# The first stage of a two-layer hybrid decoder step in two channel halves, with one group of modulation products moved in front of the first projection

## Chip, cores and metric

The kernel runs on one core of a Trainium2 chip, as a single launch. The metric is the device time of that launch in microseconds (us). Engines are named as the profile names them: PE is the tensor engine (PEld its weight loads), DVE the vector engine, ACT the scalar engine, POOL the GpSimd engine, SP the sync engine, which issues most DMAs. "ACTq" and "SPq" are the queues in which ACT and SP issue DMAs.

## The reference

Two layers run one after the other over a prompt of 512 positions and 8 single decode steps, 520 columns in all, with 1024 channels. What matters here is the beginning of a layer:

```python
mod = silu(c) @ ada_w + ada_b                 # c: 9 conditioning rows (8 samples, 1 prompt)
shift, scale, gate = split(mod, 3)
h = rms_norm(x, norm_g) * (1.0 + scale) + shift
proj = h @ w_in                               # 30 tiles of 128 columns for four mixers, then gate tiles
```

Then four mixers (RWKV-7, retention, RG-LRU, gated DeltaNet) work on slices of proj, each result is gated and lifted back to 1024 channels, the four are merged, multiplied by w_out and added to x. A last rms_norm ends the second layer. All states are written out as well. Everything is fp32, and the large products are made from two parts (a rounded part, hi, and the rest, lo): hi*hi + lo*hi + hi*lo.

## The kernel before

**Layout.** Channels lie on the 128 partitions: xT, h_hi and h_lo are [128, 8, 520], one block of 128 channels for each of the 8 middle indices. h_hi is laid over xT and h_lo over hT (`sb_parts`), so h_hi may only be written when xT is no longer needed, and xT has to be stored (scr_x) for the residual at the layer's end.

**The start (lines 346 to 470).** SP issues, in this order: the conditioning rows, the first constants, parameters, x (2 MB in four DMAs), the first two thirds of layer 0's ada_w (8 MB in eight DMAs of 1 MB, two for each of four groups b = 0..3 of 512 columns), the first three tiles of w_in into the ring (`first_load`), the store of xT in two halves, the remaining constants and the tree masks. Groups 0 and 1 are the shift of channel blocks 0 to 3 and 4 to 7, groups 2 and 3 their scale. PE transposes x into xT, sums the squares of the 8 blocks with a matrix of ones (line 458, [128,128] weights, all 128 output rows alike), and makes the four groups of modulation products (`ada_products`, line 311: 32 instructions for a group, on four column groups of 32 columns). ACT copies each group's rows out of PSUM (line 390) and PE turns them into columns (`mod_columns`, line 318). ACT also makes rs = exp(-0.5 ln(mean square + eps)) (lines 385, 387), and then the hi parts of the first two tiles of w_in (`first_split`, line 299), whose second waits for the second tile's load. When all four groups are there, DVE makes modT (line 418) and G = (1 + scale) * norm_g (line 420).

**Layer loop.** DVE makes hT = xT * G * rs for the 8 decode columns (lines 1965 to 1970) and block by block for the prompt (lines 1968, 1977), ACT adds the shift and rounds to h_hi (lines 1608, 1609), and DVE makes h_lo (lines 1974, 1980). In front of that ACT waits until the stores of xT have landed. PE makes tiles 0 and 1 of proj together, block by block: `product` splits a tile into 12 parts, 0 to 7 the blocks with the hi weights against h_hi and h_lo (line 881), 8 to 11 the lo weights (line 889), two blocks each:

```python
for p in range(KT):
    proj(0, [p])
    proj(1, [p])
for idx in range(2):
    proj(idx, range(KT, PARTS))
```

From tile 2 on PE takes a tile at a time. A weight tile is loaded by SP into one of three ring slots once the tile that had the slot is done, ACT makes its hi part (line 1540) right after it has evacuated the tile two places before (`evac`, line 1555), and POOL its lo part in two halves (line 717). All order is written out by hand: each engine's program is a fixed list, and waits are on step counters (`Track`). SP goes through the tiles in order, and `before` puts other transfers in front of given loads; in front of proj 3's load stand the wait for the last modulation step, four DMAs of a decode state and two copies of conv states (lines 526, 615, 616). After its eight h_hi steps ACT issues nine small DMAs (lines 1612 to 1620: state rows, two LoRA weights, gate weights, two small vectors), then evacuates tile 0. Both layers do this.

**Activation tables.** Where ACT needs a function that the table set loaded at that point lacks, a table load stands before the instruction. Ln and Exp follow each other in rs (lines 385 and 387 at the start, 1934 and 1936 at the join of the layers, 1926 and 1929 at the very end), in `norm` (lines 1591, 1593, three times a layer) and at lines 1657 and 1659, and each of the two has a table load of its own.

Of the kernel before, what the change touches and what calls it, by code (L numbers as in the profile page):

```python
# [4 lines left out]
D_MODEL, SEQ, DEPTH, NB = 1024, 512, 2, 8  # L5
HEADS, HD = 4, 64
# [71 lines left out]
def build_program(nc, a, o, order):  # L78
# [8 lines left out]
    with ctx:  # L87
# [52 lines left out]
        rows0 = [RC[:, b, 0:256] for b in range(4)]  # L140
        sq0 = [mg5[:, 2], mg5[:, 3], mg5[:, 4], tg[:, 1], ws[:, 14], ws[:, 15], ws[:, 16], ws[:, 17]]
# [77 lines left out]
        class Layer:  # L219

            def __init__(self, n):
                names = ("states_in", "small_weights_in", "outputs_written", "shift_rows_written", "decode_states_written", "scratch_written",
                         "decode_vectors_in", "decode_states_in", "decode_rows_in", "x_saved")
                (self.st, self.w2, self.out, self.crow, self.so, self.scr, self.vec, self.ss, self.oread, self.xout) = (sem(f"{name}{n}") for name in names)
# [120 lines left out]

        block = ctx.enter_context(nc.Block())
        @block.sync
        def _(sp):
# [9 lines left out]
            for e in range(8):  # L358
                sp.dma_start(pairs[e], a["ada_w"][0, 512 * (e % 2):512 * (e % 2) + 512, 512 * (e // 2):512 * (e // 2) + 512]  # L359
                             .rearrange("(k p) c -> p k c", p=P)).then_inc(s_ada0[e], 16)  # L360
# [15 lines left out]
        def _(act):  # L376
            A = nc.scalar.activation
            act.wait_ge(s_c, 48)
            A(mg5[0:9, 0:2, 0:512], RC[0:9, 2:4, 0:512], ACT.Tanh, scale=0.5).then_inc(*act0.step("tanh_c"))
            for d in range(KT):  # L380
                act.wait_ge(*dve0.at("x", d))
                A(sq0[d], xT[:, d, :], ACT.Square).then_inc(*act0.step("sq"))
            act.wait_ge(s_const, 32)
            act.wait_ge(*pe0.at("ss"))
            A(rs.rearrange("p (h c) -> p h c", h=2), psB[:, 2:4, 0:HALF], ACT.Ln, bias=cc("eps"), scale=1.0 / D_MODEL).then_inc(*act0.step("ln"))
# [9 lines left out]
        def _(dve):  # L395
# [17 lines left out]
            for d in range(KT):  # L413
                dve.wait_ge(*pe0.at("x", d))
                nc.vector.tensor_copy(xT[:, d, 0:SEQ], psA[:, d % 4, :]).then_inc(*dve0.step("x"))
# [2277 lines left out]
```

## Time and profile before

| | us |
|---|---|
| runs (3), median | 1380.09 |
| lowest, highest | 1377.6, 1385.19 |
| the profiled execution | 1379.26 |
| its span in the profile | 1377.4 |
| PE busy in the span | 1323.3 |
| DVE, ACT, POOL busy | 623.8, 450.6, 373.7 |

The profiled execution is one more run of the same program. Its own time is 1.9 us more than the span from its first to its last recorded instruction. In the timeline, each row is: start in us from the span's start, duration, engine, source line, operation, output<-input by the program's names, shapes, and the number of instructions merged in the row; in brackets how long the engine was idle before it and what released it. Durations of merged rows run from the first start to the last end. PE's rows overlap, since matmuls are pipelined.

### The profile page before, as it was taken

How to read it: one execution, taken by the hardware profiler on the slowest of the kernel's cores; microseconds unless marked ns; L12 is line 12 of the kernel's file. 1: busy time of each engine (PE TensorE's matmuls, PEld its weight loads, DVE VectorE, ACT ScalarE, POOL GpSimd, SP SyncE). 2: the span in 40 equal slices, each digit the busy share in tenths (PEclk: the TensorE clock that was granted, in tenths of full speed). 3: DMA queues.
4: the chain of work that ended last, by engine and by line, in shares of the span. 5: the costliest groups of instructions: out<-in, count | busy, mean ns of one | idle time of the engine just before them, and what ended most of it. 6: DMA issues, size and time to landing. Idle time of an engine off the chain costs nothing.

```text
span 1377.4 us, 39970 instructions
## 1 busy us (share of the span) xinstructions
PE 1323.3 (96%) x18146; PEld 1195.7 (87%) x18146; DVE 623.8 (45%) x1158; ACT 450.6 (33%) x742; POOL 373.7 (27%) x286
## 2 busy tenths in 40 slices
PE   6699999999999999999979999999999999999996
PEld 4699999899899999887779999999988999988795
DVE  2648514318234326656242972242543242565643
ACT  3333522234322235231143252222542223533123
POOL 0244421123222232120333442222331222322121
PEclk9899999999999999999989999999999999999998
DMA  8733231125431272578843323212273224545932
GB/s 318 237 93 89 77 95 49 44 70 123 120 85 49 64 135 82 155 194 266 284 148 91 92 78 86 59 47 64 76 165 85 64 57 90 127 132 135 291 113 93
DMA packets 275933, 162.60 MB, mean 118 GB/s; under 512 B 86102, under 2 KB 244922, under 8 KB 275252
## 3 DMA queue, kind: packets, MB, share of 16 engines
q1 hardware_dynamic: 273556, 158.01, 41.5%
q8 instruction: 143, 2.34, 0.7%
q10 hardware_dynamic: 2208, 2.03, 0.5%
q14 instruction: 26, 0.21, 0.1%
HBM read 135.25 MB, written 24.89 MB: 116 GB/s over the span
## 4 chain that ended last, share of the span: by engine, by line
PE 87%; ACT 3%; SPq 3%; DVE 3%; DMA 3%; issue 1%; ACTq 1%; DVEq 0%
PE psA L881 38%; PE psA L889 19%; PE psA L931 7%; PE psB L807 2%; PE psB L823 2%; PE psB L827 1%; DMA ring<-in_ada_w 1%; SPq L359 1%; PE psB L1006 1%; PE psB L311 1%; PE psB L1016 1%; SPq L293 1%; DMA upw<-in_w_up 1%; PE psB L791 1%; PE psB L1244 1%
## 5 line engine op out<-in xcount | busy, mean ns | idle before, releaser
L717 POOL TENSOR_TENSOR w_lo<-ring,w_hi 128x512 fp32r<-128x512 f32 x248 | 329.9, 1351 | 832.6 <-ACT w_hi L1540 790.2
L881 PE MATMUL psA<-h_hi,w_hi 128*128 128x260 f32 x1984 | 427.1, 297 | 17.7 <-DVE h_lo L1974 16.5
L881 PE MATMUL psA<-h_lo,w_hi 128*128 128x260 f32 x1984 | 402.5, 285 | 0.0
L881 PEld LDWEIGHTS psA<-h_hi,w_hi 128*128 128x128 f32 x1984 | 307.8, 190 | 37.4 <-issue 26.8
L881 PEld LDWEIGHTS psA<-h_lo,w_hi 128*128 128x128 f32 x1984 | 309.0, 190 | 0.2
L889 PE MATMUL psA<-h_hi,w_lo 128*128 128x260 f32 x1984 | 273.3, 286 | 0.0
L889 PEld LDWEIGHTS psA<-h_hi,w_lo 128*128 128x128 f32 x1984 | 248.9, 187 | 6.8 <-issue 3.0
L1540 ACT CAST w_hi<-ring 128x1024 fp32r<-128x1024 f32 x120 | 123.8, 1032 | 9.7 <-DMA ring<-in_w_in 9.6
L832 ACT COPY ws<-psB 128x128 f32<-128x128 f32 x80 | 21.5, 269 | 186.8 <-PE psB L807 159.9
L1570 ACT ACTIVATE tg<-psA 128x520 f32<-128x520 f32 x48 | 28.9, 603 | 124.8 <-PE psA L889 124.6
L840 DVE COPY_PREDICATED tg<-tmask,psB 128x128 f32<-128x128 uint8 x40 | 14.3, 356 | 101.2 <-PE psB L827 57.6
L840 DVE COPY_PREDICATED ws<-tmask,psB 128x128 f32<-128x128 uint8 x40 | 14.3, 357 | 79.0 <-PE psB L827 42.4
L717 POOL TENSOR_TENSOR rb_lo<-RB,w_hi 128x512 fp32r<-128x512 f32 x16 | 21.7, 1375 | 101.4 <-ACT w_hi L1540 101.4
L717 POOL TENSOR_TENSOR rb_lo<-RB,ra_lo 128x512 fp32r<-128x512 f32 x16 | 21.0, 1338 | 47.8 <-ACT ra_lo L1540 47.8
L931 PE MATMUL psA<-RB,upw 128*128 128x260 f32 x128 | 31.9, 393 | 1.2 <-DMA upw<-in_w_up 1.0
L1555 ACT COPY RA<-psA 128x520 f32<-128x520 f32 x18 | 10.7, 594 | 66.3 <-PE psA L889 66.3
L2229 DVE SCALAR_TENSOR_TENSOR ws<-RD,parT,ws 128x511 f32<-128x511 f32 (+2 forms) x36 | 30.9, 923 | 0.7 <-ACT ws L1744 0.6
L931 PEld LDWEIGHTS psA<-RB,upw 128*128 128x128 f32 x128 | 23.1, 190 | 9.3 <-issue 6.0
L931 PE MATMUL psA<-RA,upw 128*128 128x260 f32 x128 | 30.7, 385 | 0.0
L931 PE MATMUL psA<-RD,upw 128*128 128x260 f32 x128 | 29.9, 384 | 0.8 <-DVE RA L2030 0.8
L931 PE MATMUL psA<-RC,upw 128*128 128x260 f32 x128 | 30.0, 387 | 0.0
L889 PE MATMUL psA<-merged_hi,rb_lo 128*128 128x260 f32 x224 | 29.1, 282 | 0.0
(495 smaller groups left out, 1981.8 us busy)
## 6 DMA issues: line engine op xcount, KB each, us to landing
ring<-in_w_in SPq DMA_DIRECT2D x122, 512.0 KB, 4.2
ring<-in_ada_w SPq DMA_DIRECT2D x32, 512.0 KB, 5.6
scr_tanh<-tg SPq DMA_DIRECT2D x48, 260.0 KB, 4.6
upw<-in_w_up SPq DMA_DIRECT2D x64, 128.0 KB, 3.6
RB<-in_w_out SPq DMA_DIRECT2D x16, 512.0 KB, 3.9
RA<-scr_tanh SPq DMA_DIRECT2D x30, 260.0 KB, 4.0
ws<-scr_tanh SPq DMA_DIRECT2D x24, 260.0 KB, 4.3
xT<-scr_x SPq DMA_DIRECT2D x8, 520.0 KB, 5.1
```

The costliest lines, as they stand in the source:

```text
L293: sp.dma_start(RS[s], a["w_in"][layer, :, col:col + P].rearrange("(k p) c -> p k c", p=P)).then_inc(arrived, 16)
L717: nc.gpsimd.tensor_tensor(tile_part(RL[s][:, k], (kind, n)), tile_part(RS[s][:, k], (kind, n)), tile_part(HS[L.hslot[q]][:, k], (kind, n)) ...
L807: last = nc.tensor.matmul(meet(z0[pr, cols], lv, 0), At[pr, q, cols], meet(T4[pr, q, cols], lv, 0), start=True, stop=True)
L823: nc.tensor.matmul(meet(z0[pr, cols], lv, 0), V4[pr, q, cols], meet(Y4[pr, q, cols], lv, 0), start=True, stop=True)
L832: nc.scalar.copy(meet(q64(Y), lv, 0), meet(q64(psB[:, 2, 0:256]), lv, 0)).then_inc(*ta.step("y"))
L840: nc.vector.copy_predicated(meet(q64(T), lv, 0), bc(meet(tmask[:, lv, :], lv, 0), 1, 4), meet(q64(psB[:, 2, 0:256]), lv, 0))
L881: nc.tensor.matmul(out(h), HS[L.hslot[q]][:, p, 0:m], cols(part(p), h), start=(p == 0 and part is hi), stop=False)
L889: last = nc.tensor.matmul(out(h), RL[s][:, k, 0:m], cols(hi(k), h), start=False, stop=(k == KT - 1))
L931: last = nc.tensor.matmul(out(hf), upw[:, idx % UP_RING, i, :], outs[MERGE[idx][0]][:, i, hf * HALF:(hf + 1) * HALF], start=(i == 0), stop ...
L1540: nc.scalar.copy(tile_part(HS[L.hslot[q]], SPLIT[q]), tile_part(RS[s], SPLIT[q])).then_inc(*aw.step("hi"))
L1570: A(half(th_tile(idx)), psA[:, b:b + 2, 0:HALF], ACT.Tanh, scale=0.5).then_inc(*am.step("th"))
L2229: last = STT(out[:, t, sh:SEQ], raw[:, t, 0:SEQ - sh], par(wname, tap * n + t), out[:, t, sh:SEQ], mult, add)
```

## The change

- The start works in two halves of four channel blocks. x goes to two other places (`x0`: RC and mg5) instead of xT, so h_hi no longer lies over it, and each half is stored from there with a semaphore of its own. ACT's wait for the stores is gone from layer 0's start; SP and ACT wait for them where RC and mg5 are used again.
- Order of ada_w groups: 0, 2, 1, 3 on SP and on PE. SP's first three ring loads stand between them.
- The sum of squares: ones with 32 columns, block d on column group d % 4, then a DVE copy of the four partial sums and one more product with ones over it (the scale gets a factor 1/32).
- PE: group 0, the last product for the sums, group 2, columns of both, group 1; then, inside layer 0's loop over blocks in front of block 4, group 3, the columns of groups 1 and 3, and parts 8 and 9 of tiles 0 and 1.
- DVE makes modT, G, the decode columns and hT for each half by itself.
- POOL waits in layer 0 for h_lo of block 3 before its first lo part.
- The nine small DMAs are issued by SP in both layers, at the head of the layer's list; in layer 0 behind the wait for the last modulation step.
- ACT loads a table set (`natural_log_exp_and_others`) by hand: after the first tanh, after the squares in `norm`, before the Ln at line 1657, and after the layer's last gate tanh.

```diff
-        rows0 = [RC[:, b, 0:256] for b in range(4)]
-        sq0 = [mg5[:, 2], mg5[:, 3], mg5[:, 4], tg[:, 1], ws[:, 14], ws[:, 15], ws[:, 16], ws[:, 17]]
+        x0 = (RC[:, 0:4, :], mg5[:, 0:4, :])
+        rows0 = [RA[:, 8, 256 * (i % 2):256 * (i % 2) + 256] for i in range(4)]
+        sq0 = [ws[:, 8], ws[:, 9], mg5[:, 4], tg[:, 1], ws[:, 14], ws[:, 15], ws[:, 16], ws[:, 17]]
+        sqsum0 = ws[:, 14, :].rearrange("p (h c) -> p h c", h=2)
...
+        FIRST = (0, 2, 1, 3)
...
+        def ada0(pe, i):
+            b = FIRST[i]
+            for q in range(4):
+                if q % 2 == 0:
+                    pe.wait_ge(s_ada0[2 * b + q // 2], 16)
+                last = ada_products(bank0(i), chunks[b][q], 2 * q, q == 0, q == 3)
+            last.then_inc(*pe0.step("ada"))
...
+        def mod_rows0(act, i):
+            act.wait_ge(*pe0.at("ada", i))
+            nc.scalar.copy(rows0[i], bank0(i)).then_inc(*act0.step("modrow"))
...
+        def mod0(pe, i):
+            pe.wait_ge(*act0.at("modrow", i))
+            mod_columns(psB[:, 1, :], FIRST[i], rows0[i]).then_inc(*pe0.step("mod"))
...
+        def modulation0(dve, half):
...
+            dve.wait_ge(*pe0.at("mod", 2 * half + 1))
+            nc.vector.tensor_tensor(halves(modT[:, 0:16, :]), halves(psB[:, 1, 0:144].rearrange("p (r s) -> p r s", r=16)),
+                                    halves(bc(par("ada_b", 0, 16), 2, 9)), add).then_inc(*dve0.step("modT"))
+            dve.wait_ge(*dve0.at("modT", half))
+            nc.vector.scalar_tensor_tensor(G[:, rows, :], modT[:, 8 + 4 * half:12 + 4 * half, :], 1.0, bc(par("norm_g", 4 * half, 4), 2, 9),
+                                           add, mult).then_inc(*dve0.step("G"))
...
         def _(sp):
...
-            for n in range(RING):
-                first_load(sp, n, LAYERS[0], 0)
-            sp.wait_ge(*dve0.at("x", KT - 1))
-            for half in (slice(0, 4), slice(4, 8)):
-                sp.dma_start(scrX[:, half, :], xT[:, half, :]).then_inc(LAYERS[0].xout, 16)
+            ada_loads(0)
+            ada_loads(2)
+            first_load(sp, 0, LAYERS[0], 0)
+            ada_loads(1)
+            first_load(sp, 1, LAYERS[0], 0)
+            ada_loads(3)
+            first_load(sp, 2, LAYERS[0], 0)
+            save_x(0)
+            save_x(1)
...
         def _(act):
...
+            nc.scalar.preload_act_table_set("natural_log_exp_and_others")
             for d in range(KT):
                 act.wait_ge(*dve0.at("x", d))
-                A(sq0[d], xT[:, d, :], ACT.Square).then_inc(*act0.step("sq"))
+                A(sq0[d], x0[d // 4][:, d % 4, :], ACT.Square).then_inc(*act0.step("sq"))
...
-            for b in range(4):
-                act.wait_ge(*pe0.at("ada", 4 * b + 3))
-                nc.scalar.copy(rows0[b], psA[:, b, 0:256]).then_inc(*act0.step("modrow"))
+            mod_rows0(act, 0)
+            mod_rows0(act, 1)
             first_split(act, 0, LAYERS[0])
             first_split(act, 1, LAYERS[0])
...
         def _(dve):
...
+            dve.wait_ge(*pe0.at("ssp"))
+            nc.vector.tensor_copy(sqsum0, psB[:, 2:4, 0:HALF]).then_inc(*dve0.step("ssp"))
...
         def _(pe):
...
             for d in range(KT):
                 pe.wait_ge(*act0.at("sq", d))
+                g = 32 * (d % 4)
                 for hf in range(2):
-                    last = nc.tensor.matmul(psB[:, 2 + hf, 0:HALF], ones, sq0[d][:, hf * HALF:(hf + 1) * HALF], start=(d == 0), stop=(d == KT - 1))
+                    last = nc.tensor.matmul(psB[g:g + 32, 2 + hf, 0:HALF], ones[:, 0:32], sq0[d][:, hf * HALF:(hf + 1) * HALF], start=(d < 4), stop=(d >= 4))
+            last.then_inc(*pe0.step("ssp"))
+            ada0(pe, 0)
+            pe.wait_ge(*dve0.at("ssp"))
+            for hf in range(2):
+                last = nc.tensor.matmul(psB[:, 2 + hf, 0:HALF], ones, sqsum0[:, hf, :], start=True, stop=True)
             last.then_inc(*pe0.step("ss"))
-            for i in range(16):
-                ada0(i)
-                if i % 4 == 3 and i > 4:
-                    mod0(i // 4 - 1)
-            mod0(3).then_inc(*pe0.step("mod"))
+            ada0(pe, 1)
+            mod0(pe, 0)
+            mod0(pe, 1)
+            ada0(pe, 2)
...
                         if layer == 0:
-                            sp.wait_ge(*pe0.at("mod"))
+                            sp.wait_ge(*pe0.at("mod", 3))
+                            sp.wait_ge(L.xout[0], 16)
...
+                if layer == 0:
+                    sp.wait_ge(s_zero, 2)
+                    sp.wait_ge(*pe0.at("mod", 3))
+                sp.dma_start(srow[:, :], a["state_rows"][layer]).then_inc(s_st, 16)
+                sp.dma_start(w2[0:64, :], a["rwkv_w2"][layer]).then_inc(s_w2, 16)
+                sp.dma_start(w2[64:128, :], a["rwkv_a2"][layer]).then_inc(s_w2, 16)
...
+                    if layer == 0 and q == 0:
+                        pool.wait_ge(*dve_f.at("hl", KT // 2 - 1))
...
                 for p in range(KT):
+                    if layer == 0 and p == KT // 2:
+                        ada0(pe, 3)
+                        mod0(pe, 2)
+                        mod0(pe, 3)
+                        for idx in range(2):
+                            proj(idx, (KT, KT + 1))
                     proj(0, [p])
                     proj(1, [p])
                 for idx in range(2):
-                    proj(idx, range(KT, PARTS))
+                    proj(idx, range(KT + 2 if layer == 0 else KT, PARTS))
...
-                act.wait_ge(s_xout, 16 * (2 if layer == 0 else 3))
                 for d in range(KT):
+                    if layer == 0 and d == KT // 2:
+                        mod_rows0(act, 2)
+                        mod_rows0(act, 3)
+                    if layer and d == 0:
+                        for stored in L.xout:
+                            act.wait_ge(stored, 16)
                     act.wait_ge(*dve_f.at("hs", d))
...
-                act.dma_start(srow[:, :], a["state_rows"][layer]).then_inc(s_st, 16)
...
-                act.dma_start(gp[32:36, 1:2], a["gdn_dt_bias"][layer].unsqueeze(1)).then_inc(s_w2, 16)
                 evac(0, 1)
...
                 gates(30, 31)
+                nc.scalar.preload_act_table_set("natural_log_exp_and_others")
                 act.wait_ge(s_so, 16 * 12)
```

## Rows read from the trace of the kernel before

**Rows 1.** The page: shares of the chain that ended last, by engine

```profile
PE 87%; ACT 3%; SPq 3%; DVE 3%; DMA 3%; issue 1%; ACTq 1%; DVEq 0%
```

**Rows 2.** Timeline of the start, from the sums of squares to the first projection

```profile
20.72 2.87 PE L458 MATMUL psB<-mg,cst 128*128 128x260 f32 x12 [1.47 <-ACT ws L382]
...
27.91 1.93 PE L311 MATMUL psA<-RA,cond_padded 128*32 128x256 f32 x32
...
37.14 1.18 PE L318 MATMUL psB<-sel_halves,RC 128*128 128x18 f32 x8
...
38.67 4.92 POOL L717 TENSOR_TENSOR w_lo<-ring,w_hi 128x512 fp32r<-128x512 f32 x4 [36.95 <-ACT w_hi L299]
...
42.38 1.77 DVE L1968 SCALAR_TENSOR_TENSOR hT<-xT,G,tg 128x512 f32<-128x512 f32 x1
...
46.06 0.72 ACT L1609 ACTIVATE h_hi<-hT,modT 128x512 fp32r<-128x512 f32 x1 [5.68 <-DMA scr_x<-xT]
...
47.99 0.77 PE L881 MATMUL psA<-h_hi,w_hi 128*128 128x260 f32 x2 [9.66 <-DVE h_lo L1974]
```

**Rows 3.** Windows (length; busy time and instructions of each engine; PEclk; DMA share; GB/s)

```profile
40.00:43.00 3.00, 0.00 (x0) 0.00 (x0) 2.71 (x4) 0.38 (x1) 3.00 (x3) 0.74 1.02 427
...
49.00:52.00 3.00, 3.00 (x16) 3.00 (x16) 3.00 (x6) 1.71 (x3) 0.00 (x0) 0.55 1.04 361
```

**Rows 4.** Chain in order of time, then ACT's timeline

```profile
47.18 0.66 DVE h_lo L1974
...
62.50 4.07 PE psA L881 x32
...
55.17 0.59 ACTq L1612 DMA_DIRECT2D ws<-in_state_rows  x1
...
60.82 0.59 ACT L1555 COPY RA<-psA 128x520 f32<-128x520 f32 x1 [4.93 <-PE psA L889]
```

**Rows 5.** SP's issues, landing times of RB (ada_w) and line 293 (ring), ACT's cast

```profile
8.77 4.33 SPq L359 DMA_DIRECT2D RB<-in_ada_w  x2
...
23.56 11.90 SPq L293 DMA_DIRECT2D ring<-in_w_in  x3
...
40.21 3.26 SPq L526 DMA_DIRECT2D RC<-in_state_rwkv_wkv  x4
...
DMA to landing us min/median/max: 13.0/13.8/14.6
...
DMA to landing us min/median/max: 9.2/13.1/14.0
...
39.34 1.04 ACT L299 CAST w_hi<-ring 128x1024 fp32r<-128x1024 f32 x1 [0.74 <-DMA ring<-in_w_in]
...
ws<-in_tree_masks SPq DMA_DIRECT2D x1, 896.0 KB, 15.5
```

**Rows 6.** DMAs until 70 us: issues of proj 3's load, median us to landing

```profile
ring<-in_w_in SPq DMA_DIRECT2D x2, 16.0 KB, 2.5
```

**Rows 7.** Timeline of the join of the two layers

```profile
709.24 1.14 PE L1471 MATMUL psB<-ws,cst 128*128 128x260 f32 x4 [1.11 <-ACT ws L1919]
...
711.43 0.69 ACT L1934 ACTIVATE tg<-psB,cst 128x520 f32<-128x520 f32 x1
...
712.14 1.28 ACT L1936 ACT_TABLE_LOAD   x1
...
714.32 0.75 DVE L1968 SCALAR_TENSOR_TENSOR hT<-xT,G,tg 128x512 f32<-128x512 f32 x1
...
717.21 0.77 PE L881 MATMUL psA<-h_hi,w_hi 128*128 128x260 f32 x2 [6.83 <-DVE h_lo L1974]
...
731.46 0.48 PE L881 MATMUL psA<-h_hi,w_hi 128*128 128x260 f32 x2 [0.39 <-ACT w_hi L1540]
```

**Rows 8.** Timeline of the end, last sums and the table load for Exp

```profile
1365.75 0.20 PE L1523 MATMUL psB<-cst,ws 128*8 128x1 f32 x2
...
1366.63 1.28 ACT L1929 ACT_TABLE_LOAD   x1
```

More of the change, by code:

```diff
@@ L344, in build_masks, with bank0 @@
             nc.vector.tensor_scalar(selg[0:4, :, 2:4], sel2[0:4], 0.5, None, mult).then_inc(*dve0.step("tmask"))
+        FIRST = (0, 2, 1, 3)
+        def bank0(i):
+            return (psA[:, 0, 0:256], psA[:, 1, 0:256], psB[:, 0, 0:256], psB[:, 3, 0:256])[i]
+        def ada0(pe, i):
[12 more added lines that the diff above has]
+        def modulation0(dve, half):
+            rows = slice(4 * half, 4 * half + 4)
+            halves = lambda ap: ap.rearrange("p (x r) s -> p x r s", x=2)[:, :, rows, :]
+            dve.wait_ge(*dve0.at("parT"))
+            dve.wait_ge(*pe0.at("mod", 2 * half + 1))
[4 more added lines that the diff above has]
+                                           add, mult).then_inc(*dve0.step("G"))
+            dve.wait_ge(*dve0.at("G", half))
         block = ctx.enter_context(nc.Block())
@@ L401, in _ @@
             dve.wait_ge(*pe0.at("xs"))
-            nc.vector.tensor_copy(xT[:, :, SEQ:TT], psB[:, 0, 0:64].rearrange("p (d b) -> p d b", d=KT)).then_inc(*dve0.step("xs"))
+            for half in range(2):
+                last = nc.vector.tensor_copy(x0[half][:, :, SEQ:TT], psB[:, 0, 32 * half:32 * half + 32].rearrange("p (d b) -> p d b", d=4))
+            last.then_inc(*dve0.step("xs"))
             dve.wait_ge(*pe0.at("c"))
@@ L442, in _ @@
             pe.wait_ge(*dve0.at("parT"))
-            def ada0(i):
-                b, q = i // 4, i % 4
-                pe.wait_ge(s_ada0[i // 2], 16)
-                ada_products(psA[:, b, :], chunks[b][q], 2 * q, q == 0, q == 3).then_inc(*pe0.step("ada"))
-            def mod0(b):
-                pe.wait_ge(*act0.at("modrow", b))
-                return mod_columns(psB[:, 1, :], b, rows0[b])
             pe.wait_ge(*dve0.at("selh"))
@@ L481, in build_program @@
             turned = ws[:, 0:8, :].rearrange("p (t a) c -> p t a c", a=2)
+            h_parts = ((0, KT // 2), (KT // 2, KT)) if layer == 0 else ((0, KT),)
             def ada_bank(b):
@@ L667, in before @@
                         sp.dma_start(o["s_lru_h"][layer], hrow[1:9, :]).then_inc(s_out, 16)
+                if layer == 0:
[4 more added lines that the diff above has]
+                sp.dma_start(w2[64:128, :], a["rwkv_a2"][layer]).then_inc(s_w2, 16)
+                for g in range(2):
+                    for hf in range(2):
+                        sp.dma_start(gw[hf * HD:(hf + 1) * HD, 2 * g:2 * g + 2, hf * HD:(hf + 1) * HD],
+                                      a["lru_gate_w"][layer, g].rearrange("(i f) d e -> f d i e", f=2)[hf]).then_inc(s_w2, 16)
+                sp.dma_start(gp[32:36, 0:1], a["gdn_A_log"][layer].unsqueeze(1)).then_inc(s_w2, 16)
+                sp.dma_start(gp[32:36, 1:2], a["gdn_dt_bias"][layer].unsqueeze(1)).then_inc(s_w2, 16)
                 follows = {x: y for x, y in zip(L.prev[RING:], RINGSEQ[RING:]) if x is not None and x in PLACE and PLACE[x] < PLACE[y]}
@@ L1637, in _ @@
                 act.wait_ge(*pa.at("crow"))
+                if layer == 0:
+                    act.wait_ge(L.xout[1], 16)
                 nc.scalar.copy(crowA[:, 0:512], psB[0:11, 0, :])
```

92 lines of the change are left out of this document (46 added, 46 removed).

## The prediction

> **What bounds the kernel now.** First the chain that ended last: 87% of the span lies on TensorE (PE) [rows 1]. In such a kernel time comes only from places where PE stands still, or from the last microseconds. The timeline and the table by windows show three: the start, the join of the two layers near 712, the tail. The change touches all three.
>
> The start, in the timeline [rows 2]: sums of squares from 20.72 to 27.9; sixteen steps of modulation products, in groups of 32 matmuls at 1.93; the last mods end at 38.32 (37.14 + 1.18), and for 9.66 us PE issues nothing. DVE has its factors by then, but ScalarE (ACT) may not start h_hi, which lies over xT, until the store of xT has landed: 46.06. PE's first product comes 1.93 later, at 47.99. In the windows [rows 3] the granted clock is 0.74 in 40 to 43 and 0.55 in 49 to 52. That is a fall from 2.4 to 1.2 GHz at 41.4, some 3.1 us after the last matmul, and the return at 51.7, 3.7 after the first product. It costs nothing here, because DVE sets the pace: 0.66 for each h_lo and each hT, 1.33 per channel block, against 1.0 for PE's eight matmuls [rows 4]. At the end ACT issues nine DMAs from 55.17, so the copy of proj 0 comes at 60.82 and proj 2 starts at 62.50 [rows 4]. What follows is PE bound until the join.
>
> **When the loads land** [rows 5]. Issue plus landing time: the third and fourth megabyte of ada_w at 21.8 (8.77 + 13.0) and 24.4 (issued at 9.8, 14.6 to land), so 2.7 us each; ring tile 0 at 37.6 (23.56 + 14.0); the cast of ring tile 1 waited for its data until 39.34, so 1.8 a tile. In the new order (two, two, ring 0, two, ring 1, two, ring 2) the scale of the first half lands at 24.4, ring 0 at 26.2, the shift of the second half at 31.6, ring 1 at 33.4, the scale of the second half at 38.8. The bytes in front of the masks are the same, so these still land near 54.5 (issued at 39, 15.5 to land).
>
> **The change at the start.** Sums of squares: 32 full-width instructions in 7.2 become 32 of 32 columns, a DVE copy of 0.7 and four full ones, 0.9. With four column groups side by side the 32 would take 1.9, as the modulation products do; with none, 7.2. The calls come two to a group in turn, so I take 1.9 to 5.4, where one instruction in four overlaps. Then group 0 (1.93), the ss step, group 2 and two mods (1.2): mods 0 and 1 end at 28.5 to 32. ACT no longer stops twice for a table, rs is there by 27 to 30.5, and DVE could offer hT of block 0 by 31 to 34.6. But ACT makes both first casts before it touches h, and the second waits for ring 1: 33.4 + 1.05 gives **34.45** for h_hi. That cover hides the sums up to 5.4; without overlap h_hi comes 2 us later.
>
> By the old distance of 1.93 PE starts at 36.4. Block 3's h_lo ends five DVE steps later, 39.7. PE had group 1 until 32.6 and then 3.8 us of nothing, so by [rows 3] the clock falls, and here it counts: 16 matmuls in those 3 us make 1.7 to 1.8 a block, against DVE's 1.33. I take it as fallen, for two blocks: block 3 ends at 41.9 (at the high level 40.7). Group 3 takes 1.9 and the last two mods 1.1: **mod 3 at 44.9** (43.7). Then modT, G, hg, hr. Old, beside POOL, the mods' end to the first hT took 4.06 (38.32 to 42.38); that hT took 1.77 beside POOL and 0.75 alone [rows 2, 7], so 4.06 shrinks to 1.7 by that ratio, less on smaller tiles: 1.3. From the first hT to PE's product it is 2.9 at the join (714.32 to 717.21). The new wait holds POOL until 39.7; its four halves of 1.23 end at 44.6, before modT. So block 4 starts at 49.0; PE fills the gap with the first lo parts (2.0). Block 7 ends at 53.3 (3.3 + 1.0), proj 0 at 54.3. Behind it wait ACT's copy and cast 2, no longer behind DMA issues: 1.68, as from 60.82 to 62.50. Proj 2 starts at **56.0** instead of 62.50: **6.5 us**.
>
> Moved to SP: nine small DMAs, which held ACT from 55.17 to 60.8, 5.6 us. SP has them from 44.9 to 50.5, then six more at 0.8 each (four in 3.26 before [rows 5]) until 55.3, and is a microsecond late for proj 3's load. That lands in 2.5 [rows 6], and its cast is due at 61.8, one tile after 56.0: covered by three microseconds. Their data queue behind the masks and arrive near 55; DVE reaches the masks at 52.3 and waits 2.2. The constants behind that wait release ACT near 58, whose next evacuation is due at 61.8 as well. If this cover went, each microsecond past it would be one for PE.
>
> **The join** [rows 7]. PE's last sum ends at 710.38 (709.24 + 1.14); Ln starts at 711.43 behind a table load, Exp behind another of 1.28. With one set loaded before, 1.0 + 1.3 = 2.3. Against it: POOL's two halves behind the last cast run to 712.6, now beside hr and the first hT: 0.6. The nine DMAs go from ACT here too, and PE's wait of 0.39 for the cast with them. Together **2.1**. SP issues them while PE stands anyway. A tanh later needs a load of 1.28, in front of an evacuation that has a tile's 5.8 us for its 1.7.
>
> **The tail** [rows 8]. The sum ends at 1365.95. Exp's load of 1.28 begins 0.68 later, with two short Ln in between, so some 0.2 of that is Ln's own load still running: **1.5**. The other preloads (three norms a layer, the Ln of line 1657) spare 1.28 on chains for which PE has projections to do; I cost them at nothing, and they would cost 1.28 each where a tanh with its load came to be waited for.
>
> Sum: 6.5 + 2.1 + 1.5 = 10.1 against the profiled 1379.26 (span 1377.4, 1.9 around it): **1369.2**. The median of the runs, 1380.09, is 0.8 above that execution, within their spread.
>
> **What a switch of tables costs.** Ln ends at 712.12 and the load for Exp starts at 712.14: no drain to be seen in front of it, and 1.28 for itself [rows 7]. The Trainium skill, page "ScalarE: Activation LUTs", section "What ACT_TABLE_LOAD costs", gives 1.28 and a drain of 1.38 more for each switch; by that join and tail would give 2.8 more. The trace doesn't bear it out.
>
> **Rivals.**
> 1. *A switch costs double.* If the two Exp loads that leave the path took another 1.28 each with them, 12.7 is gained: 1366.6. The 0.02 speaks against it. Chance 0.03. It is the rule of the page above.
> 2. *The middle of the start stalls.* Sums without overlap (2 later), POOL beside the second half's factors (up to 2.8, the 4.06 against 1.3): the start gives 1.7 to 4 and the whole 5.3 to 7.6: 1373. For it: the handover PE, ACT, PE, DVE, ACT, DVE, PE now comes twice. Against: POOL is done by 44.6. Chance 0.19.
> 3. *The preload spares nothing.* No row shows one set that serves both; today every pair has two loads. Then 6.5 + 0.4 = 6.9, 1372.4. Chance 0.06.
> 4. *SP becomes the bound: slower.* Fifteen issues stand between mod 3 and the load of proj 3. With full rings two ada loads took 4.33 [rows 5], 2.2 each; fifteen end at 77.9, and issue 1.0, landing 2.5 and cast make 81.6 for a cast due at 61.8: 19.8 late, less 10.1, so 1389. It turns slower from 1.5 an issue (15 in 44.9 to 68.1). Against: SP's four at 40.21 took 0.8 with the same backlog. Chance 0.03. The Trainium skill, page "DMA: Bandwidth & Descriptors", section "Issuing engines are not separate DMA queues", says that spreading issues over engines saves only the sequencers' issue time; the change gives just that up, and the 5.6 us on ACT agree.
>
> **Numbers.** The forecast's case has 0.69; its own range is 1366 (the clock stays up, 1.2, and loads a microsecond early) to 1372. This kernel's measurement can tell about 0.5%, 6.9 us, from no change: faster is below 1373.2. That holds for the forecast, 1, most of 3 and half of 2: 0.82; same 0.15; slower 0.03. The range 1364 to 1375 takes in 1 to 3 and leaves out 4 and what I haven't seen.
>
> **What would show it.** Cast 1 waiting for its DMA until 33.4, h_hi at 34.5, PE at 36.4 with the clock at half, mod 3 at 44.9, block 4 at 49.0, proj 2 at 56.0; no load between Ln and Exp at join and tail; nine SP issues of 0.6. I am wrong if h_hi starts late for want of hT, if proj 3's cast waits for a DMA, or if time after 62.5 gives the gain back.

## The result, and the profile after

The changed kernel takes 1369.01 us in the median of 8 runs (seven of them lie between 1366.11 and 1371.09), the kernel before beside it 1376.89 (1375.42 to 1385.19). One run of the changed kernel (4743.71) and one of the last experiment (2080.0) were disturbed and enter no ratio and no range given here. The ratio is 0.9931, 95% interval 0.9909 to 0.9954: 6 to 13 us faster. The profiled execution took 1368.49, with a span of 1366.6, so 10.8 less than before between spans; forecast were 10.1. The sum came near, but its first term did not: the start gave 4.1 in this trace, not 6.5, and 2.5 to 2.8 came from a place that no step of the change touches. That the total agrees is in this part luck.

The start, which answers to [rows 2] and [rows 4]. (All four groups of modulation products stood in front of the first projection before. What moved is the last of them, to between blocks 3 and 4, and none was moved to the front, as the title could be read.) First the timeline of the changed kernel:

```profile
21.36 1.12 PE L498 MATMUL psB<-ws,cst 128*32 128x260 f32 x16
...
27.08 1.18 PE L322 MATMUL psB<-sel_halves,RA 128*128 128x18 f32 x8
...
34.38 1.04 ACT L303 CAST w_hi<-ring 128x1024 fp32r<-128x1024 f32 x1 [5.84 <-DMA ring<-in_w_in]
...
35.33 0.72 ACT L1683 ACTIVATE h_hi<-hT,modT 128x512 fp32r<-128x512 f32 x1
...
37.19 0.77 PE L942 MATMUL psA<-h_hi,w_hi 128*128 128x260 f32 x2 [2.62 <-DVE h_lo L2034]
...
43.04 1.93 PE L315 MATMUL psB<-ws,cond_padded 128*32 128x256 f32 x32
...
44.91 1.18 PE L322 MATMUL psB<-sel_halves,RA 128*128 128x18 f32 x8
...
49.73 0.51 PE L942 MATMUL psA<-h_hi,w_hi 128*128 128x260 f32 x2 [1.63 <-DVE h_lo L2034]
...
55.57 2.07 PE L950 MATMUL psA<-h_hi,w_lo 128*128 128x260 f32 x16
...
58.41 0.48 PE L942 MATMUL psA<-h_hi,w_hi 128*128 128x260 f32 x2 [0.77 <-ACT w_hi L1607]
```

The chain is the one forecast: ring tile 1 lands, ACT casts it, h_hi, h_lo, PE. The sums of squares are over by 22.5 (they take 2.0, as the estimate for four column groups side by side had it), and the first half's columns by 28.3. Then everybody waits for ring tile 1. PE's first product comes 10.8 before that of [rows 2]; at proj 2, which started at 62.50 [rows 4], 4.1 of it are left. The windows of the same execution (columns as in [rows 3]) show where PE lost:

```profile
32.00:35.00 3.00, 1.93 (x16) 0.59 (x16) 0.00 (x0) 0.62 (x1) 0.00 (x0) 0.50 1.06 373
35.00:38.00 3.00, 0.81 (x4) 0.84 (x5) 1.81 (x4) 2.04 (x5) 0.00 (x0) 0.50 1.06 375
38.00:41.00 3.00, 3.00 (x15) 3.00 (x15) 2.45 (x4) 1.45 (x3) 0.34 (x1) 0.50 1.13 390
...
50.00:53.00 3.00, 2.90 (x18) 2.70 (x18) 2.87 (x5) 1.45 (x2) 0.00 (x0) 0.76 1.06 269
53.00:56.00 3.00, 3.00 (x19) 3.00 (x19) 0.99 (x5) 0.00 (x0) 0.00 (x0) 0.67 1.04 208
```

The seventh number, those in brackets not counted, is the granted clock as a share of 2.4 GHz. From 31.1 to 41.3 it is at the low level of 1.2 GHz: from 38 to 41, 15 rows of matmuls fill three microseconds. It falls a second time at 51.4, for 3.4, while blocks 4 to 7 are made. That one was in no row of before.

The join, against [rows 7], in the timeline of the changed kernel:

```profile
702.40 1.14 PE L1538 MATMUL psB<-ws,cst 128*128 128x260 f32 x4 [1.10 <-ACT ws L1986]
...
703.59 0.69 ACT L2001 ACTIVATE tg<-psB,cst 128x520 f32<-128x520 f32 x1 [0.30 <-PE psB L1538]
704.31 0.64 ACT L2003 ACTIVATE tg<-tg 128x520 f32<-128x520 f32 x1
...
705.05 0.88 DVE L2043 TENSOR_TENSOR hT<-hT,tg 128x64 f32<-128x64 f32 x1 [2.90 <-ACT tg L2003]
705.85 0.74 DVE L2044 SCALAR_TENSOR_TENSOR hT<-xT,G,tg 128x512 f32<-128x512 f32 x1
...
708.73 0.77 PE L942 MATMUL psA<-h_hi,w_hi 128*128 128x260 f32 x2 [5.18 <-DVE h_lo L2034]
```

No table load stands before or between Ln and Exp, and the first hT comes 3.45 after the sum's start instead of 5.08 [rows 7]. POOL now overlaps DVE, and the small product before the first hT takes 0.88. The tail, against [rows 8]:

```profile
1356.57 0.20 PE L1590 MATMUL psB<-cst,ws 128*8 128x1 f32 x2
1356.80 0.26 ACT L1993 ACTIVATE rs_col<-psB,cst 128x4 f32<-128x4 f32 x1 [1.59 <-PE psB L1590]
...
1357.23 0.21 ACT L1996 ACTIVATE rs_col<-rs_col 128x4 f32<-128x4 f32 x1
```

Exp follows directly. The page's chain that ended last, against [rows 1]: 90% on PE instead of 87%.

```profile
PE 90%; DMA 3%; DVE 2%; ACT 2%; SPq 2%; issue 1%; ACTq 0%; DVEq 0%
```

### The profile page after: what moved, and what is told of

Read it like the earlier page. It is cut to its first block, busy times and chain, and to the rows that moved or that the text cites. A ratio compares the mean times of both kernels' runs of the same rounds, so it can differ in the third digit from the quotient of the medians.

```text
span 1366.6 us, 39992 instructions
## 1 busy us (share of the span) xinstructions
PE 1318.0 (96%) x18150; PEld 1190.6 (87%) x18150; DVE 623.3 (46%) x1166; ACT 450.7 (33%) x742; POOL 375.0 (27%) x286
## 3 DMA queue, kind: packets, MB, share of 16 engines
q10 hardware_dynamic: 544, 1.05, 0.2%
## 4 chain that ended last, share of the span: by engine, by line
PE 90%; DMA 3%; DVE 2%; ACT 2%; SPq 2%; issue 1%; ACTq 0%; DVEq 0%
PE psA L942 40%; PE psA L950 20%; PE psA L992 8%; PE psB L884 2%; PE psB L868 2%; DMA ring<-in_ada_w 2%; PE psB L888 1%; PE psB L1073 1%; PE psB L315 1%; PE psB L1083 1%; DMA ring<-in_w_in 1%; SPq L400 1%; PE psB L852 1%; PE psB L1311 1%; PE psB L800 1%
## 5 line engine op out<-in xcount | busy, mean ns | idle before, releaser
L992 PEld LDWEIGHTS psA<-RB,upw 128*128 128x128 f32 x128 | 23.2, 190 | 9.5 <-issue 4.9
```

The source lines that it names most:

```text
L992: last = nc.tensor.matmul(out(hf), upw[:, idx % UP_RING, i, :], outs[MERGE[idx][0]][:, i, hf * HALF:(hf + 1) * HALF], start=(i == 0), stop ...
```

## The experiments

A "trace of after" is a profiled execution of the changed kernel. "Cast n" and "the cast of proj n" are the starts of ACT's rounding of weight tile n; "proj 2 starts" is PE's first product with tile 2, the end of the first stage.

**Each kernel once more.** Where do 2.5 us at layer 0's end come from, and is the second fall of the clock part of the change?

> The kernel before, once more. Question: the two traces differ by 4.1 us at the start, 2.0 at the join, 1.4 at the tail, and by 2.5 to 2.8 between 666 and 700, at layer 0's end, which no step of the change explains. Theory A (scatter of a stretch that waits for loads): in this trace layer 0's end moves by itself against the first trace of before, by one to three us, while ring tile 1's cast, proj 2, join and tail stand within 0.5. Theory B (the change itself sped that stretch up): both traces of before agree there within 0.5, and both of after too.

> The changed kernel, once more. Theory A (layer 0's end is scatter): against its first trace the stretch from 666 to 700 moves by one to three us. Theory B (an effect of the change): within 0.5. At the start both expect cast 1 at 34.4 within 0.5, the first product near 37.2, the clock at half from there to 41.4 and again for some three us while blocks 4 to 7 are made, proj 2 at 58.4. If the second fall is missing here, it is scatter of its own and proj 2 starts near 56.

Own times 1378.63 and 1367.15. To compare places I take the start of ACT's cast of a given tile in each trace. From that of tile 59 (near 565) to that of tile 69 (near 690), a stretch in which PE waits for loads of ada_w, the two traces of before take 127.3 and 126.7, the two of after 125.6 and 126.2. The first pair differs by 1.7 there, the second by 0.5. At tile 69 the two traces of one and the same kernel before are 2.7 apart: 2.1 had built up ahead of tile 59, 0.6 in the stretch. Theory A, then, though the scatter lies less in this stretch than all along the layer. A part of it can be seen in the granted clock. In the first trace of before it falls at 686 for 3.4 us, behind two waits for loads:

```profile
685.00:690.00 5.00, 4.53 (x28) 4.12 (x29) 0.00 (x0) 0.14 (x1) 0.00 (x0) 0.66 0.84 271
```

The first trace of after has no fall between 366 and 706, the two second traces have one each in this stretch. At half clock 3.4 us cost up to 1.7, which is the whole difference of the first pair.

In the second trace of after the start matches (cast 1 at 34.05, first product 36.86), and there is no second fall:

```profile
50.00:53.00 3.00, 2.54 (x17) 2.13 (x17) 2.87 (x6) 1.45 (x2) 0.00 (x0) 1.00 1.05 242
53.00:56.00 3.00, 3.00 (x26) 3.00 (x26) 2.00 (x6) 0.00 (x0) 0.00 (x0) 1.00 0.90 196
```

Yet proj 2 starts at 57.76, not at 56: a gain of 4.7. Block 4 started 0.54 later than in the first trace, and proj 2 0.65 earlier, so the second fall cost 1.2 in the first trace.

**The four preloads taken out of the changed kernel.**

```diff
-            nc.scalar.preload_act_table_set("natural_log_exp_and_others")
```

(and the three others).

> The changed kernel without the four loads by hand of a table set. Theory (the preloads are worth their loads on the path and nothing elsewhere): at the start nothing, as the casts wait for ring tile 1 until 34.4 and the factors of the norm are ready with two loads of 1.28 more by 30; at the join the load in front of Ln costs 0.3 to 1.0 and that for Exp 1.3, so 1.6 to 2.3; at the tail 1.3 to 1.5. In all 2.9 to 3.8 slower than the changed kernel, ratio to the kernel before near 0.9957. Rival (the three norms and the L-chain of the first mixer count too): 1.28 for each of some, so 5 to 9 slower. Rival (a switch costs its drain as well, 2.66): 5 to 6 slower, with gaps of over a microsecond in front of each load.

Ratio to before 0.9954 (0.9937 to 0.9971), so 3.2 slower than the changed kernel, with an interval for this difference of about 0 to 7. Cast 1 comes at 34.30: nothing at the start. The join in its timeline:

```profile
706.35 1.28 ACT L1997 ACT_TABLE_LOAD   x1
...
707.64 0.69 ACT L1997 ACTIVATE tg<-psB,cst 128x520 f32<-128x520 f32 x1
708.35 1.28 ACT L1999 ACT_TABLE_LOAD   x1
709.65 0.64 ACT L1999 ACTIVATE tg<-tg 128x520 f32<-128x520 f32 x1
710.39 0.23 DVE L2039 TENSOR_TENSOR hT<-hT,tg 128x64 f32<-128x64 f32 x1 [5.18 <-ACT tg L1999]
```

From the cast that opens the join to the cast after proj 0 it takes 26.86, the changed kernel 25.36 and 25.23, the kernel before 27.45 and 27.42. The loads are worth 1.5 to 1.6, and there are two of 1.28 with 0.02 in front of the second. The tail, from the last cast to the end, is 25.0 here, 25.0 and 24.7 in the two traces of before, 23.6 and 23.2 in the changed kernel: 1.4 to 1.8. Together 3.1 by the traces, and 3.2 by the times. The rival with a drain falls by the 0.02. The rival in which the norms count too (5 to 9) is not excluded by the times alone, since their interval reaches into it; what speaks against it is only that join and tail make up the middle of the difference. The profiled execution was 8.7 longer, with 6.8 us more at the low clock; one profile can't tell such a difference.

**The small DMAs given back to ACT**, in both layers:

```diff
-                sp.dma_start(srow[:, :], a["state_rows"][layer]).then_inc(s_st, 16)
...
+                act.dma_start(srow[:, :], a["state_rows"][layer]).then_inc(s_st, 16)
...
                 evac(0, 1)
```

> The changed kernel with the nine small DMAs of each layer issued by ACT again, behind h_hi of block 7. Theory (ACT's 5.6 of issuing stood in front of the copy of proj 0): copy of proj 0 at 58.5 to 59 instead of 56.1 to 56.7, as block 7's h_hi ends near 52.6 and nine issues take 5.6 to 6, so proj 2 1.5 to 2.2 later, near 60; at the join 0.4 later. Rival (free either way): under 0.5 at both places.

ACT's timeline:

```profile
51.13 0.59 ACTq L1673 DMA_DIRECT2D ws<-in_state_rows  x1
...
56.65 0.26 ACTq L1681 DMA_DIRECT2D gp<-in_gdn_dt_bias  x1
56.96 0.59 ACT L1609 COPY RA<-psA 128x520 f32<-128x520 f32 x1 [5.11 <-PE psA L937]
```

The issues run from 51.13 to 56.91, beside the last h_hi and not behind it. PE's lo parts of tile 0 begin at 55.00, and ACT's copy, which in the two traces of after starts 1.16 behind them, starts 1.96 behind them here, at 56.96. Most of the issues cover time in which that tile isn't ready anyway: PE waits 1.57 for cast 2 instead of 0.77. That is 0.8, where I expected 1.5 to 2.2; proj 2 starts at 58.64, 0.2 later than in the trace of after that has the same two falls of the clock, 0.9 later than in the other. At the join the same stretch takes 25.79 instead of 25.3: 0.5, as expected, though other traces without this edit go up to 25.6. With the preloads' 1.5 this makes up the join's 2.1.

**The sums of squares at full width again.**

```diff
-                    last = nc.tensor.matmul(psB[g:g + 32, 2 + hf, 0:HALF], ones[:, 0:32], sq0[d][:, hf * HALF:(hf + 1) * HALF], start=(d < 4), stop=(d >= 4))
+                    last = nc.tensor.matmul(psB[:, 2 + hf, 0:HALF], ones, sq0[d][:, hf * HALF:(hf + 1) * HALF], start=(d == 0), stop=(d == KT - 1))
```

> The changed kernel with the 32 matmuls of the sum of squares at full width again (the later product over the four parts stays, its scale adapted). Theory (hidden behind ring tile 1): the sums take 7.2 instead of 2.0, the first half's columns end at 33.4 instead of 28.3, the first hT at 34.5 to 35.1, h_hi at 35.3 to 35.8 where cast 1 had ended at 35.4: proj 2 moves by 0 to 0.5. PE's work in 20 to 35 has fewer holes, so the clock may stand longer: then blocks 0 to 3 gain up to 1.5 from it and proj 2 is earlier. Rival (the sums are on the path): proj 2 later by 2 to 5.

PE's timeline:

```profile
32.56 1.18 PE L322 MATMUL psB<-sel_halves,RA 128*128 128x18 f32 x8
33.67 1.93 PE L315 MATMUL psB<-RB,cond_padded 128*32 128x256 f32 x32
37.48 0.48 PE L942 MATMUL psA<-h_hi,w_hi 128*128 128x260 f32 x2 [1.87 <-DVE h_lo L2034]
42.16 1.93 PE L315 MATMUL psB<-ws,cond_padded 128*32 128x256 f32 x32
...
56.55 0.48 PE L942 MATMUL psA<-h_hi,w_hi 128*128 128x260 f32 x2 [0.77 <-ACT w_hi L1607]
```

Five microseconds more work for PE, and proj 2 starts 1.2 and 1.9 *earlier* than in the two traces of after. PE stands 1.87 in front of its first product instead of 2.62 and more before it, the granted clock is 1.00 in every window from 26 to 59, and blocks 0 to 3 take 4.7 where they took 5.9. What the change cut out of the sums was hidden anyway but for 0.3 to 0.6, and the idle time it left cost the clock.

**Matmuls of constants in PE's gaps.** If that reading is right, any work in the gaps must do it.

```diff
+        def keep_busy(bank, n):
+            for _ in range(n):
+                nc.tensor.matmul(bank, ones, cst[:, 0:HALF], start=True, stop=True)
...
+            keep_busy(psA[:, 3, 0:HALF], 11)
```

> The changed kernel, with matmuls of constants (128x260, results unused) put into four of PE's gaps in the first stage: 7 in front of each half of the third group of modulation products, 11 behind it, 7 in front of block 4. Theory (the half clock of blocks 0 to 3 comes from PE standing from 28.3 on, and costs 1.5 to 2 on the path; the second fall, which one trace of the changed kernel has at 51.4 and the other lacks, costs 1.2): the clock stays at 1.00 from 26 to 59, block 3 ends near 41.3 instead of 42.9 to 43.8, last columns of the modulation done at 44.4 instead of 46.1 to 46.6, proj 2 at 55.4 to 56 instead of 57.8 to 58.4. Rival (the clock falls all the same, or DVE, 1.33 a block, sets the pace anyway): proj 2 not before 57.4.

The clock stood at 1.00 from 26 to 59, and proj 2 came at 59.80, *later* than without. The filler (these matmuls of constants) had been sized by a wrong price:

```profile
27.86 3.31 PE L376 MATMUL psA<-cst 128*128 128x260 f32 x14
...
36.37 5.09 PE L376 MATMUL psA<-cst 128*128 128x260 f32 x22
```

Seven calls are 14 rows and take 3.3, so 0.46 a call: I had divided the 7.2 of the old sums by 32 rows, and there are two rows to a call. The first product had to wait until 41.10. With 3, 3, 5 and 3 calls:

> As e5_busy with fewer calls, since each takes 0.46 and not 0.22 as I had reckoned (14 rows in 3.23): 3, 3, 5 and 3 in the four gaps, so that none runs past its gap. Theory (half clock costs 1.2 to 1.9 in the first stage; e7_full_sums had proj 2 at 56.55 with the clock up): the clock is at 1.00 from 26 to 59, block 3 ends at 41.7 to 42.1, proj 2 starts at 56.0 to 56.6, against 57.8 to 58.6 in four traces without such work. Rival (in e7_full_sums something else brought it): proj 2 at 57.8 or later.

```profile
33.57 2.46 PE L376 MATMUL psA<-cst 128*128 128x260 f32 x10
37.12 0.48 PE L949 MATMUL psA<-h_hi,w_hi 128*128 128x260 f32 x2 [1.09 <-DVE h_lo L2043]
...
56.21 0.47 PE L949 MATMUL psA<-h_hi,w_hi 128*128 128x260 f32 x2 [0.76 <-ACT w_hi L1616]
```

Proj 2 at 56.21, in the range expected, with the clock at 1.00 throughout. The low clock costs the changed kernel 1.6 (against 57.76, one fall) to 2.2 (against 58.41, two falls). That the clock goes by PE's gaps here doesn't hang on two traces: in all six traces in which the gaps of the start are left open (the two of after, no preloads, DMAs on ACT, and the next two experiments) it falls between 30 and 32.5, and in all six in which they are filled, by the full sums or by constants, it stands at 1.00 from 26 to 59. The whole time shows none of this: the one run with full sums took 1367.64, that with the right filler 1367.02, among the changed kernel's 1366.11 to 1371.09.

**POOL's wait taken out.**

```diff
-                    if layer == 0 and q == 0:
-                        pool.wait_ge(*dve_f.at("hl", KT // 2 - 1))
```

> The changed kernel without POOL's wait for h_lo of block 3, so that its lo parts of tiles 0 and 1 run right behind the casts, at 28.6 and 35.4, beside DVE's factors and h_lo. Theory (POOL beside DVE stretches DVE's steps, as 1.77 for an hT of 0.75 before): h_lo and hT of blocks 0 and 1 take 0.9 to 1.8 each instead of 0.66, the first product comes 0.5 to 1 later, DVE's step for block 3 ends up to 2 later; as PE makes blocks 0 to 3 at half clock and is 2.4 behind DVE there, the end of block 3 moves by under 1: proj 2 later by 0 to 1. Rival (the wait is needed): 1.5 to 2.5 later. Rival (the wait was for nothing, the steps keep 0.66): no change at any step.

DVE's timeline:

```profile
28.46 1.14 DVE L2039 TENSOR_TENSOR hT<-RC,G 128x32 f32<-128x32 f32 x1
29.63 1.20 DVE L2041 TENSOR_TENSOR hT<-hT,tg 128x32 f32<-128x32 f32 x1
...
36.07 0.62 DVE L2049 TENSOR_TENSOR h_lo<-hT,h_hi 128x32 fp32r<-128x32 f32 x1 [3.81 <-ACT h_hi L1680]
36.62 1.80 DVE L2032 SCALAR_TENSOR_TENSOR h_lo<-hT,modT,h_hi 128x512 fp32r<-128x512 f32 x1
```

Beside POOL (28.26 to 30.78 and 35.38 to 37.87) products of 32 columns take 1.14 and 1.20 instead of 0.19, the h_lo 1.80 instead of 0.75. The first product is 1.4 to 1.7 late (38.56), and proj 2 comes at 59.31, 0.9 and 1.55 later than in the traces of after. This trace has no second fall of the clock, so the like to compare it with is the second trace of after, which has none either: 1.55, at the lower end of the rival's 1.5 to 2.5, and not the theory's 0 to 1. The wait is worth about 1.5, as far as one trace on each side can tell.

**Ring tile 1 first.** ACT's second cast waits for this tile, and a group of products that isn't needed until block 4 is loaded in front of it.

```diff
-            ada_loads(1)
-            first_load(sp, 1, LAYERS[0], 0)
+            first_load(sp, 1, LAYERS[0], 0)
+            ada_loads(1)
...
-            ada0(pe, 2)
...
                     if layer == 0 and p == KT // 2:
+                        ada0(pe, 2)
                         ada0(pe, 3)
```

> The changed kernel with ring tile 1 loaded in front of the second half's shift, and that group of products made with the last group, between blocks 3 and 4. Theory (the first stage waits for ring tile 1, then for the chain PE, ACT, DVE of the second half): cast 1 comes 5.4 earlier, at 29.0, h_hi at 30.1 where the first hT now sets it, first product at 32, block 3's end near 37 to 38, last columns of the modulation at 42.5 to 43 instead of 46.1, proj 2 some 3 us earlier, at 55 to 55.5; the whole 3 us faster than the changed kernel, 0.991 of before. Rival (the load of the last group, 38.8 plus one us, bounds the middle): last columns not before 43, gain 2 to 3. Rival (half clock takes it: PE has longer gaps between few products): the clock is at half for most of the stretch to 55 and the gain is under 1.5.

Ratio 0.9894 (0.9867 to 0.9922). Cast 1 at 28.8, first product 32.40, columns done at 43.57, proj 2 at 54.71, 3.1 and 3.7 earlier than in the traces of after. That is the theory, with the columns 0.6 late behind blocks at half clock. But at the cast of proj 4 the gain was 1.2 and 1.8. The same with filler, too much of it first:

> Ring tile 1 loaded in front of the second half's shift, as in e4_ring1_first, with 16 matmuls of constants behind the first half's columns and 7 in front of block 4. Theory (the clock's fall at 30 to 37 is the rest of the loss): the clock stays up, block 3 ends near 36.8 instead of 38.7, then the last group's load is waited for until 40 at most, last columns at 42 to 42.3 instead of 43.6, proj 2 at 53.2 to 53.6 instead of 54.7. The whole against the kernel before: 0.988 to 0.990 if the stretch at layer 0's end, which waits for its loads, passes the gain on; 0.992 if that stretch takes it back. Rival (only the loads bound the middle): proj 2 at 54.5.

Ratio 0.991 (0.988 to 0.994). 16 and 7 calls were too many again (sized by the same wrong price): first product 35.30, proj 2 at 55.76. Then with 7 and 3 calls:

> As e8_ring1_busy with 7 and 3 calls instead of 16 and 7. Theory: first product at 32.4 as in e4_ring1_first, clock up, block 3's end at 37.0 instead of 38.7, last group waits for its load until 40 at most, last columns at 42.0 to 42.8 instead of 43.6, proj 2 at 53.2 to 54.0 instead of 54.7 there and 57.8 to 58.4 in the changed kernel. The whole 4 us below the changed kernel if layer 0's end passes it on: ratio to the kernel before 0.988 to 0.991; if that stretch takes it back, 0.993.

Ratio 0.9918 (0.9896 to 0.994). First product 32.41, proj 2 at 53.36, 5.0 before that of the profiled changed kernel, and the whole no faster than the two before it. Timeline:

```profile
53.36 0.47 PE L946 MATMUL psA<-h_hi,w_hi 128*128 128x260 f32 x2 [0.76 <-ACT w_hi L1614]
...
60.71 0.24 ACT L1614 CAST w_hi<-ring 128x64 fp32r<-128x64 f32 x1 [7.00 <-DMA ring<-in_w_in]
...
61.09 0.40 PE L946 MATMUL psA<-h_hi,w_hi 128*36 128x260 f32 x2 [1.75 <-ACT w_hi L1614]
```

Proj 3's load was issued at 51.67 and kept ACT waiting until 60.7, whose next evacuation stood behind it, and PE for 1.75. Over the traces:

| | proj 2 starts | cast of proj 3 | cast of proj 4 |
|---|---|---|---|
| before | 62.50 | 63.07 | 69.15 |
| after, two traces | 58.41, 57.76 | 59.98, 60.15 | 65.07, 64.40 |
| full sums | 56.55 | 59.88 | 63.21 |
| filler, right size | 56.21 | 59.87 | 62.85 |
| ring 1 first, much filler | 55.76 | 59.52 | 62.41 |
| ring 1 first | 54.71 | 60.58 | 63.23 |
| ring 1 first, filler | 53.36 | 60.71 | 62.92 |
| and a late store | 53.85 | 57.42 | 60.49 |

Up to the last row the cast of proj 3 stands like a wall: wherever proj 2 starts between 53.4 and 58.4, it comes at 59.5 to 60.7. The cast of proj 4 has to be read with more care. Where nothing holds it, it follows the start of proj 2 by 6.65: so in before, both traces of after, full sums, filler of the right size, ring 1 first with much filler, and the last row. Above the last row, only the two with proj 2 below 55 lose to the wall, 1.9 and 2.9. ACT with the right filler, then with ring 1 first:

```profile
62.23 0.59 ACT L1631 COPY RA<-psA 128x520 f32<-128x520 f32 x1 [1.39 <-PE psA L957]
...
62.85 1.05 ACT L1616 CAST w_hi<-ring 128x1024 fp32r<-128x1024 f32 x1
...
63.23 1.05 ACT L1607 CAST w_hi<-ring 128x1024 fp32r<-128x1024 f32 x1 [1.23 <-DMA ring<-in_w_in]
```

The last row moves the wall:

```diff
             save_x(0)
-            save_x(1)
...
+                    elif (kind, n) == ("proj", 6) and layer == 0:
+                        sp.dma_start(scrX[:, 4:8, :], x0[1]).then_inc(L.xout[1], 16)
```

> e9_ring1_busy_half with the store of the second half of x (1040 KB) issued in front of proj 6's load instead of in front of the tree masks. In e9_ring1_busy_half and e4_ring1_first the gain at proj 2 (5.0 and 3.7) is only 2.2 and 1.8 at the cast of proj 4, as the cast of proj 3 waits for its load until 60.7 and 60.6, whenever proj 2 starts. Theory (the load of proj 3 waits behind what was issued before it): a megabyte less in front of it, 2.7, so the masks arrive 2.7 earlier, the cast of proj 3 comes at 58.0 instead of 60.7, PE's wait for it goes from 1.75 to 0 to 0.2, and the cast of proj 4 comes at 60.5 to 61.2 instead of 62.9: 2 us more than e9_ring1_busy_half and 4 more than the changed kernel. Ratio to the kernel before 0.988 to 0.991. Rival (proj 3's load is bound by the many small packets issued right ahead of it, not by the bytes): cast of proj 3 stays at 60 or later, and the ratio near 0.992 as before.

```profile
53.85 0.47 PE L947 MATMUL psA<-h_hi,w_hi 128*128 128x260 f32 x2 [0.77 <-ACT w_hi L1615]
...
57.42 0.25 ACT L1615 CAST w_hi<-ring 128x64 fp32r<-128x64 f32 x1 [3.23 <-DMA ring<-in_w_in]
...
60.49 1.05 ACT L1615 CAST w_hi<-ring 128x1024 fp32r<-128x1024 f32 x1
```

A megabyte out of the way brings proj 3's cast to 57.4, and proj 4's to 60.49, 4.6 and 3.9 before the traces of after and 2.4 before the same kernel with the store in its old place, with no wait of PE for these casts. Proj 3's load was issued at 52.16 behind the same small transfers as before and landed 4.1 after its issue in the median of its two DMAs, instead of 7.8: it was the bytes in front, and not the packets. The ratio is 0.9897 (0.9877 to 0.9916), with times from 1362.88 to 1367.54: the fastest of the study beside "ring tile 1 first" alone. Its interval overlaps a little with that of the changed kernel, and 0.9897 can't be told from 0.9894: the 4 us are shown at the cast of proj 4, in the traces; that they reach the end is likely and not shown.

## Why the prediction was right, and where not

**The start, 6.5 forecast, 4.1 and 4.7 measured.** The mechanism was right and the term mis-sized; that the whole fits to 0.7 all the same is luck, since other places gave what this one lacks. Ring tile 1: 34.38 and 34.05 instead of 33.4. From cast to h_hi to PE the steps held (0.95 and 1.86 instead of 1.05 and 1.93). The blocks were the error. I took the clock as fallen "for two blocks", at 1.7 to 1.8 each. The price was right: pairs of rows, four to a block, stand 0.43 apart. But they do so until 41.4 and 42.7 in the two traces, for two and a half and three and a half blocks, so blocks 0 to 3 took 5.9 and 6.7 where I had 5.5. From there to block 4 it was 6.7, and I had 7.1. Blocks 4 to 7 I had paced by DVE at the high clock, 4.3: with a second fall they took 5.8, without it 4.7. Added up with the first product, 0.8 and 0.5 late, and 0.1 behind block 7, that is the 2.4 and 1.8 that are missing. The clock took 1.6 to 2.2, as the filler of the right size shows. I had also laid the fall to 3.8 us of nothing behind group 1. It came earlier, at 31.1 and 32.3, before or just as PE began the second half of that group, for whose load it had waited; the gap in front of the first product was 2.62 and 2.94. My range named a case with the clock up (1.2 better), not one with it down longer.

**The sums of squares.** I took a middle, 1.9 to 5.4; it was 2.0. That they are hidden was right; that the time taken off them comes back as idle time with a price was in none of my steps.

**SP's queue.** Nine issues from 46.19 to 51.8, six more to 55.1, near the 44.9 to 50.5 and 55.3 forecast. DVE waited 2.01 for the masks in the first trace of after and 0.98 in the second (2.2). One of the signs named for being wrong did show: the cast of proj 3 waited for its DMA, 1.22 and 2.04, as the load landed later than the 2.5 of [rows 6] allowed. It cost PE nothing, and the cast of proj 4 came 6.65 behind proj 2 as before. "Covered by three microseconds" was too much, then, but some cover was there, and the table shows it going: with proj 2 at 54.71 PE waits 0.25 for proj 3's cast, at 53.36 1.75.

**The join, 2.1; measured 2.1 and 2.2.** Table loads 1.5 net (2.3 less the 0.6 for POOL beside hr, where the trace has 0.65), the DMAs 0.5. **The tail, 1.5; measured 1.4 and 1.5.**

**Behind 62.5** the first pair of traces gives 3.2 more, 2.5 to 2.8 of it at layer 0's end, which made a sum of 7.6 into 10.8. The second pair gives 3.1 more, but 1.1 of it before the join and 1.9 in layer 1. In both pairs the trace of before spends 10.2 us more at the low clock behind the start than that of after, which at half clock costs up to 5.1, so falls can account for it. Whether the change has a part in them is open. Over all traces the stretch from cast 59 to 69 takes 126.7 to 127.3 in the three without preloads and 123.2 to 127.9 in the eleven with them, 127.0 and 125.6 in the mean. That looks like a gain from the preloads in the norms, but falls sort the traces better: the six with a fall in this stretch take 126.2 to 127.9, the eight without one 123.2 to 126.6, and among the six those with preloads (126.8 in the mean) and without (127.0) hardly differ.

**Rivals.** A table switch costs 1.28 and no drain (number 1 fell). The chances themselves were added up wrong: 0.69, 0.03, most of 0.06 and half of 0.19 make about 0.86 and not 0.82. Number 2, "the middle of the start stalls", said 1.7 to 4 for the start, from sums without overlap and POOL; neither happened, though the size came near. Number 3 fell by the preload experiment. Number 4, SP as the bound, needed 1.5 an issue; it was 0.6.

## What to carry to other kernels

Time that you take off hidden work on the tensor engine is not free: if it leaves the engine idle in front of a stretch that it bounds, look at the granted clock of that stretch, and price it at the low level for longer than the first two blocks. Before you move a start forward, list what is loaded behind it in the same queues: the first load that lands at a fixed time, here proj 3's, is where the gain ends, and moving the bytes in front of it gave 2.4 us two tiles later. None of this is proven at the end of the kernel, where other scatter is as large. And count calls, not rows of a view, before you size work by them.

## What was not expected of the hardware

- **The clock falls while PE is at work.** In one trace of after it fell at 51.4, 1.7 into blocks 4 to 7, behind a gap of 1.63; in the other, with the same gap, it stayed up. Without preloads it fell in the same place (0.69 in 50 to 53), and with the DMAs on ACT (from 50.8 for 3.4).
- **Falls come and go between executions of the same program**, mostly for 3.4 us each. Summed over windows of 5 us, behind the start and away from the join, the first trace of before has two from 365 to 385, one at 685 and one at 1035; its second trace has one at 665 and two from 1040 to 1050; the first of after has one at 360, the second one at 660. Six timed runs of "ring 1 first, filler" agree with it: mean granted clock 0.993 with 1363.09 us, 0.988 with 1369.09. Five thousandths of 1366 us are 13.7 us at half clock, which would cost 6.8 if PE had work all the while; the times differ by 6.0. That would be most of the spread of this kernel's times. The places are not arbitrary: all falls of the fourteen traces away from start and join lie at 357 to 383, 659 to 690 and 1024 to 1049. Those at 686 and 660 come behind waits of PE for loads. At 365 and 1035 the rows show no gap ahead, but work of one kind: each of the falls of the first and the third stretch comes within five microseconds behind the start of four products whose input lies on 4 partitions (1.98 for the four, line 1208 before, 1275 after). They run four times in every trace, and a fall follows in fewer than half of the cases; what decides it stays open.
- **POOL beside DVE** stretches the smallest products most: 0.19 became 1.14 and 1.20 where POOL's halves take 1.23 each, and an h_lo of 0.75 became 1.80.
